# Weights fetched as pairs of chunks, one transfer of 2 MB in place of two of 1 MB

## What is computed

```python
def swiglu(h, w_in, w_down):
    a, b = jnp.split(h @ w_in, 2, axis=-1)
    return (jax.nn.silu(a) * b) @ w_down
...
    u = jnp.take(expert_u, ic, axis=0)
    a = jnp.einsum('td,thkd->thk', xc, u)
    w = (gc * jax.nn.gelu(a, approximate=False)).astype(xc.dtype)
    v = jnp.take(expert_v, ic, axis=0)
    return jnp.einsum('thk,thkd->td', w, v)
```

## Time and profile before

| | |
|---|---|
| median of 3 runs | 3406.84 us (3400.28 to 3407.38) |
| the profiled execution | 3398.3 us, its span 3396.5 us |
| PE busy | 2978.7 us, 88% of the span |
| DVE, ACT, POOL busy | 68%, 41%, 14% |
| moved by DMA | 640.27 MB, mean 189 GB/s |
| mean granted clock of TensorE | 0.939 |

### The profile page before, as it was taken

How to read it: one execution, slowest core, us unless ns; L and a number is a source line. 1 busy time by engine, 2 the same in 40 slices (tenths; PEclk the granted TensorE clock), 3 DMA queues, 4 the chain that set the end, 5 groups by cost and what they waited for, 6 DMA issues and landing times.

```text
span 3396.5 us, 48223 instructions
## 1 busy us (share of the span) xinstructions
PE 2978.7 (88%) x18518; PEld 2623.3 (77%) x18518; DVE 2309.9 (68%) x3190; ACT 1376.6 (41%) x1424; POOL 462.5 (14%) x244
## 2 busy tenths in 40 slices
PE   4998359999894599747999999999979999999999
PEld 3887147878784488626999998878768999998887
DVE  6887568875777555565797885556565978865565
ACT  3444234444444244323444344444434444344443
POOL 0300002202000011000485000000001880000000
PEclk9999569999997799968999999999989999999999
DMA  6786026765770145402455665667534555665675
GB/s 243 286 290 241 0 80 235 281 221 174 272 279 12 50 168 170 145 0 97 164 186 183 218 213 204 220 243 279 184 136 150 185 185 195 221 216 196 237 273 209
DMA packets 146886, 640.27 MB, mean 189 GB/s; under 512 B 12456, under 2 KB 46288, under 8 KB 90320
## 3 DMA queue, kind: packets, MB, share of 16 engines
q1 hardware_dynamic: 126928, 567.92, 48.4%
q10 hardware_dynamic: 19840, 70.79, 5.8%
HBM read 604.04 MB, written 34.62 MB: 188 GB/s over the span
## 4 chain that ended last, share of the span: by engine, by line
PE 80%; DVE 11%; DMA 4%; ACT 3%; issue 2%; SPq 0%; DVEq 0%; ACTq 0%
PE pp L443 23%; PE pp L445 11%; PE pp L581 7%; PE pp L582 7%; PE pp L583 7%; PE mz L647 6%; PE mz L649 6%; PE mz L650 6%; PE mz L623 3%; DMA raw<-expert_v 2%; DVE gsq L1136 2%; PE pp L491 1%; DVE w_lo L1039 1%; DMA ada_raw<-ada 1%; ACT w_hi L768 1%
## 5 line engine op out<-in xcount | busy, mean ns | idle before, releaser
L1039 DVE TENSOR_TENSOR w_lo<-raw,w_hi 128x2048 fp32r<-128x2048 f32 (+1 forms) x422 | 924.5, 2191 | 472.1 <-ACT w_hi L768 471.6
L768 ACT ACTIVATE w_hi<-raw 128x2048 fp32r<-128x2048 f32 (+1 forms) x486 | 894.0, 1840 | 557.6 <-DMA raw<-expert_v 370.7
L443 PE MATMUL pp<-hs,w_hi 128*128 128x512 f32 x2400 | 868.4, 406 | 41.1 <-DVE hs L1089 41.0
L445 PE MATMUL pp<-hs,w_lo 128*128 128x256 f32 x2400 | 679.6, 283 | 0.0
L443 PEld LDWEIGHTS pp<-hs,w_hi 128*128 128x128 f32 x2400 | 458.2, 191 | 166.3 <-issue 45.0
L581 PE MATMUL pp<-hs,w_hi 128*128 128x256 f32 x2048 | 585.5, 286 | 0.0
L582 PE MATMUL pp<-hs,w_hi 128*128 128x256 f32 x2048 | 579.9, 283 | 0.0
L583 PE MATMUL pp<-hs,w_lo 128*128 128x256 f32 x2048 | 579.8, 283 | 0.0
L1578 POOL TENSOR_TENSOR w_lo<-raw,w_hi 128x2048 fp32r<-128x2048 f32 x64 | 319.3, 5001 | 1157.3 <-ACT w_hi L768 1157.3
L445 PEld LDWEIGHTS pp<-hs,w_lo 128*128 128x128 f32 x2400 | 463.9, 193 | 0.0
L443 PE MATMUL pp<-us,w_hi 128*128 128x512 f32 x960 | 347.4, 406 | 80.2 <-DVE us L1147 74.5
(11 more groups left out here) (246 smaller groups left out, 3204.6 us busy)
## 6 DMA issues: line engine op xcount, KB each, us to landing
raw<-expert_u SPq DMA_DIRECT2D x128, 1024.0 KB, 4.9
raw<-expert_v SPq DMA_DIRECT2D x128, 1024.0 KB, 4.9
raw<-ffn_in SPq DMA_DIRECT2D x88, 1024.0 KB, 4.9
ada_raw<-ada ACTq DMA_DIRECT2D x120, 512.0 KB, 5.5
raw<-ffn_down SPq DMA_DIRECT2D x64, 704.0 KB, 5.0
raw<-out_w SPq DMA_DIRECT2D x16, 1024.0 KB, 4.9
raw<-hgrn SPq DMA_DIRECT2D x16, 1024.0 KB, 5.1
raw<-query SPq DMA_DIRECT2D x16, 1024.0 KB, 4.9
```

Of the source, the lines that this page charges most:

```text
L443: mm(outp, w_hi[:, slot, a:a + P], rhs[:, k0 + k].rearrange("p a t -> p (a t)"), start=(k0 + k == 0), stop=False, skip_group_check=True)
L445: last = mm(outp[:, 0:T], w_lo[:, slot, a:a + P], rhs[:, k0 + k, 0, :], start=False, stop=(k0 + k == last_k), skip_group_check=True)
L768: f(w_hi[:, slot, 0:n], raw[:, slot, 0:n], ACT.Copy).then_inc(hi_ready, 1)
L1039: v.tensor_tensor(w_lo[:, slot, 0:n], raw[:, slot, 0:n], w_hi[:, slot, 0:n].bitcast(F32), ALU.subtract)\
```

## The change

A load brings both chunks of a pair. SP waits until both chunks of the pair before last are used, and issues one transfer into the two slots. There is one semaphore for each half of the buffer instead of one for each slot, and ScalarE waits for it ahead of the first chunk of the pair only.

```diff
-        landed = [sem(f"landed{i}") for i in range(SLOTS)]
+        landed = [sem(f"landed{i}") for i in range(SLOTS // 2)]
...
-                    for j in range(2):
-                        c = 2 * pair + j
-                        if not isinstance(c, int) or c >= SLOTS:
-                            sp.wait_ge(w_used, c - SLOTS + 1)
-                        src = source[ph.kind][ph.index]
-                        sp.dma_start(raw[:, 2 * half + j, 0:n], src[bass.ds(2 * rp + j, 1)]).then_inc(landed[2 * half + j], 16)
+                    if not isinstance(pair, int) or pair >= SLOTS // 2:
+                        sp.wait_ge(w_used, 2 * pair - 2)
+                    src = source[ph.kind][ph.index][bass.ds(2 * rp, 2)].rearrange("c p n -> p c n")
+                    sp.dma_start(raw[:, 2 * half:2 * half + 2, 0:n], src).then_inc(landed[half], 16)
...
-                act.wait_ge(landed[slot], 16 * (lap + 1))
+                if j == 0:
+                    act.wait_ge(landed[half], 16 * (lap + 1))
```

## The result

The changed kernel takes 4242.34 us (median of 4 runs, 4237.13 to 4256.05) against 3404.47 us for the kernel before in the same comparison. The ratio is 1.2469, 95% interval 1.2443 to 1.2496. The profiled execution took 4238.52 us, its span is 4236.7 us, 840.2 more than before.

A forecast was written before the change was run, and what follows sets the result against it. TensorE was taken to be busy all through, with the load path covered but not by much. Stage losses of 774 us, 603 in expert_v, on 3398.3 gave 4172, and 8.5 for the median gave 4180 us; range 3960 to 4300.

The forecast's parts named there:

- the phase ends behind ffn_down: At four ffn_down ends, the next phase's first split delays the last add to x and the norm by some 4.8 us.
- products with ada: ffn_in 0 and 1, attn, hgrn: landing 8.7 us beside ada's transfers, 1.2 us more a pair, 34 us in all.
- The loop in expert_v: w_split queues behind the next pair's weights, a serial loop: 18.2 us a pair for 11.1, TensorE idle 7.1; with clock, 603 us.
- The clock: In expert_v, TensorE at half clock for 5.0 us after each gap, losing 2.5 us a pair.
- The hand-overs: Passing work between queues, from SP's issue and from landing to ScalarE and on, takes about 0.4 us together.
- The landing: One 2 MB weight transfer lands in 7.4 us, against 4.9 for 1 MB; 8.7 with ada beside it.
- (A + B)/2: Products, ffn_down, even expert_u: time per pair, A from load issue to the next split ready, B the pair's own work.
- Faster: Rival: the fixed 2.4 us is paid once for two chunks and expert_v's weight waits go: 3342 us, chance 0.03.
- hidden: Rival: time the same as the kernel before, chance 0.03.
- The clock rival: The clock stays up in expert_v's gaps of 7 us: 152 us less, 4028 us, chance 0.12.
- Half the loss in expert_v: Rival: queues not held up as claimed, activations' split gets ahead or lookahead covers more: about 3880 us, chance 0.10.
- Landings were slower: Rival: 2 MB lands in 8.7 us, 1.3 more a pair in expert_v: about 165 us more, 4345 us, chance 0.10.

The follow-up runs named there:

- after_ahead: Changed kernel with expert_v's activations split one chunk ahead, before the next pair's weights in the queues of ScalarE and VectorE: 3752.19 us, ratio 1.1012.
- late_1mb: Kernel before, with both chunks of a pair loaded as late as in the changed kernel, but by two 1 MB transfers: 3867.78 us, ratio 1.1351.
- filler: Changed kernel with 24 extra unused matmuls in TensorE's gap before each pair's second chunk in expert_v: 4239.62 us, ratio 1.2443.
- filler30: Changed kernel with 30 extra unused matmuls in TensorE's gap before each pair's second chunk in expert_v: 4145.76 us, ratio 1.2188.

## Why the prediction was right

4180 was forecast, 3960 to 4300, and 4242 measured. By the profiled executions 774 us were forecast and 840.2 came. By stages, from the length of each in the trace:

| part | forecast | measured | of it in slower matmuls |
|---|---|---|---|
| expert_v, 4 stages | 603 | 145.8 + 154.9 + 149.3 + 139.1 = 589 | 123 |
| expert_u even, 2 stages | 50 | 34.3 + 40.3 = 75 | 24 |
| expert_u odd | 2 | 4 | 3 |
| ffn_down | 37 | 66 | 19 |
| the phase ends behind ffn_down | 19 | -7 | |
| products with ada | 34 | 55 | 20 |
| products without | 15 | 25 | 8 |
| out phases, to the next norm's end | 14 | 22 | 2 |
| attentions, HGRN, start and other gaps | 0 | 11 | |

The last column is TensorE's busy time in the stages after, less that before, for the same matmuls.

**The loop in expert_v** held in its form: the order swap opens it, the matmul that waits once a pair waits for w_split, the gap is 7.5 us for 7.1. Inside it two terms missed in opposite directions. The landing is 7.8 us, not 7.4, which over 61 pairs is 24 us more. The clock costs 1.6, not 2.5, 55 us less. The hand-overs came as forecast: from the end of the pair before, at 2378.26, to TensorE's start at 2391.28 are 13.0 us, 7.8 of it the landing and 5.2 the queues and hand-overs, for 5.25 in the forecast. That would make 572 us; the 17 that are left to 589 stay open. The sum was met more closely than its terms, by misses that cancel. For the clock I took half clock for 5.0 us, the middle of 3.4 and 6.5; the rows above show 3.9 behind the gap, and the clock had already fallen within the gap (0.80 as its mean). The 6.5 of the earlier trace rows were those of a norm, where TensorE waits for hs between its matmuls as well.

**The landing** was off by 0.4 us where nothing runs beside the load. The four loads in a row were read as 2.5 us for each further megabyte, but they landed 2.6, 2.4 and 3.0 apart, 2.7 on average, and in the profile after the second megabyte costs 2.9. With ada beside them the loads of ffn_in 0 and 1 land in 8.7 us, as forecast, and those of attn and hgrn in 9.3 and 9.2. So the landing does not explain ffn_in 0, before and after:

```profile
57.90:183.10 125.20, 125.16 (x704) 108.97 (x704) 100.60 (x139) 60.73 (x70) 41.29 (x42) 0.98 0.72 261
```

```profile
59.00:201.30 142.30, 132.19 (x704) 111.78 (x704) 101.31 (x139) 62.30 (x71) 41.18 (x42) 0.95 0.63 224
```

17.1 us where 9 pairs x 1.2 = 11 were forecast. Of the 17.1, 10.1 are idle time of TensorE, and 7.0 are the same 704 matmuls taking longer, 132.2 us for 125.2, at a clock of 0.95 for 0.98. The Trainium skill's fit (DMA: Bandwidth & Descriptors, anatomy of one DMA), which its page gives for loads issued from GpSimd, gave an estimated 6.8 us for 2 MB; the 2 MB loads here, issued from SP, take 7.8 us in expert_v, and the rows' 7.4 was nearer.

**The clock outside expert_v** is the term that was left out: the forecast had it at nothing, because the gaps there were to be short. The last column of the table has it at 71 us in the products, ffn_down and the even expert_u stages. Without it the path's form (A + B)/2 fits: of the 75 us of expert_u even 51 are left for 50 forecast, of the products with ada 35 for 34, of those without 17 for 15, of ffn_down 47 for 37. The form says nothing on how the stall is shared out between pairs, and in the trace it is not shared: pairs start without a gap, until one waits for all of it. TensorE before, in and behind one of these gaps in expert_u 0:

```profile
1918.00:1921.50 3.50, 3.50 (x30) 3.31 (x28) 3.29 (x10) 3.50 (x3) 1.97 (x1) 1.00 0.01 2
1921.50:1924.20 2.70, 0.02 (x1) 0.00 (x0) 2.70 (x1) 0.75 (x2) 2.70 (x2) 0.96 0.54 103
1924.20:1927.40 3.20, 3.16 (x15) 3.17 (x16) 3.03 (x9) 0.00 (x0) 3.20 (x1) 0.50 1.01 428
1927.40:1930.80 3.40, 3.40 (x30) 3.40 (x30) 3.16 (x12) 1.36 (x1) 2.25 (x1) 1.00 0.32 133
```

2.7 us idle, and then half as many matmuls for 3.2 us, 1.6 us lost. A gap of 3.0 us in the same stage, a little earlier, is followed by 28 matmuls in 3.4 us at full clock:

```profile
1894.90:1897.90 3.00, 0.02 (x1) 0.00 (x0) 2.72 (x14) 1.04 (x2) 3.00 (x2) 1.00 0.53 126
1897.90:1901.30 3.40, 3.36 (x28) 3.37 (x29) 3.09 (x16) 0.00 (x0) 3.40 (x1) 1.00 1.01 429
```

expert_u 2, where the granted clock is lower, loses more:

```profile
3119.50:3344.40 224.90, 199.65 (x1541) 198.25 (x1540) 151.07 (x413) 79.79 (x66) 146.41 (x31) 0.92 0.38 140
```

These 71 us are read from the traces; no run took the clock out of these stages.

**The phase ends** behind ffn_down were forecast 19 us longer and came 7 us shorter, which hides part of ffn_down's own miss in the sum. Why is not shown.

**The rivals.** Faster and hidden are out: the fixed part of a transfer was saved 243 times, on a path where it had been covered. The clock rival is measured at 97 us, not 152, and the clock did not stay up. Half the loss in expert_v would have needed w_split to get ahead of the weights in the queues; after_ahead shows what that is worth, but the change has no such edit. Landings were slower by 0.4 us, of the 1.3 of that rival.

## What to carry to other kernels

A buffer's depth in chunks is not what covers a load. Write down the path from "slot free" through landing and every engine that prepares the data, and see at which chunk the load can start; fetching two chunks at once takes one chunk out of that, and adds the second one's transfer. Then look at what else stands in the preparing engines' queues behind the wait: something that needs nothing from the transfer, as w_split here, turns a stall that two buffers share into a serial one, and the order of two instructions was worth 490 us on the kernel after the change and 10 on the one before it. What a larger transfer saved here was the time of issuing, and an idle SP said that this limited nothing.

## What the runs showed of the hardware

The clock fell after gaps much shorter than I had believed to matter. It fell behind 4.6 us of idle time (late_1mb), behind 2.7 (expert_u 0), and behind 2.0 that followed 5.5 us of work (filler), while a gap of 0.8 left it up (filler30). Each time the next matmuls ran at 1.2 GHz for 3 to 4 us and lost 1.6 to 1.9. The length of the gap alone does not decide it: one of 3.0 us in expert_u 0 left the clock up. The Trainium skill (TensorE: Matmul & The Clock Gate, HAM oscillation) describes the clock falling between bursts that wait for a DMA; the traces agree, and show it for gaps of 2 to 3 us too, though not for each of them. A 2 MB transfer cost 2.9 us more than one of 1 MB, although four of 1 MB in one queue had landed 2.7 us apart on average.
